# Three quarters of the up projection by Strassen's scheme in a decoder step on one core

## The reference

```python
x = layer_norm(DN_ALPHA * x + cross_attn(x, mem_k, mem_v, xq_w, xo_w), ln2_g, ln2_b)
f = jnp.square(jax.nn.relu(x @ w1 + b1)) @ w2 + b2      # w1 1024 x 4096, w2 4096 x 1024
x = layer_norm(DN_ALPHA * x + f, ln3_g, ln3_b)
```

## Time and profile before

| | us |
|---|---|
| three runs, median | 1382.69 |
| lowest and highest | 1379.11, 1385.63 |
| profiled execution, its own time | 1379.41 |
| its span | 1377.6 |
| PE busy in it | 1326.0 |
| first up slab's Relus to the last one's | 655.1 to 1010.2 |
| down units, first and last matmul with 264 columns | 1009.9 to 1264 |

### The profile page before, as it was taken

The page is one execution under the profiler, slowest core; times in us unless marked ns, Lnnn a source line. Parts: engine busy times, 40 slices in busy tenths (PEclk is TensorE's granted clock), DMA queues, the critical chain, the costliest instruction groups (busy, mean ns, idle before and its releaser), DMA issues.

```text
span 1377.6 us, 21845 instructions
## 1 busy us (share of the span) xinstructions
PE 1326.0 (96%) x8744; PEld 1279.3 (93%) x8744; DVE 882.5 (64%) x1034; ACT 431.9 (31%) x821; POOL 783.7 (57%) x576
## 2 busy tenths in 40 slices
PE   6999999999999999999999999999999999989995
PEld 6999988788899978889999999999999999989995
DVE  5899994456612762387664246324469998897767
ACT  4223442245612441145211131112243444422233
POOL 3476987544933714629433337333359999994522
PEclk9999999989999999999999999999999999999998
DMA  8222452110020266201233433333343133346112
GB/s 257 69 51 45 126 162 78 31 46 1 32 61 31 76 234 239 80 16 46 79 93 93 156 93 93 93 93 140 140 162 109 58 110 125 110 158 206 57 47 81
DMA packets 59018, 136.91 MB, mean 99 GB/s; under 512 B 21568, under 2 KB 27968, under 8 KB 56512
## 3 DMA queue, kind: packets, MB, share of 16 engines
q1 hardware_dynamic: 49184, 132.99, 29.7%
q10 hardware_dynamic: 9760, 2.93, 0.9%
HBM read 107.02 MB, written 28.88 MB: 99 GB/s over the span
## 4 chain that ended last, share of the span: by engine, by line
PE 62%; DVE 27%; issue 3%; POOL 3%; DMA 2%; ACT 2%; SPq 0%; DVEq 0%; ACTq 0%; POOLq 0%
PE bank L809 20%; PE bank L810 19%; PE bank L811 19%; DVE bank L1901 11%; DVE ffn_sum L2404 2%; POOL w_low L759 2%; DVE form_low L2372 1%; DVE weight_sums L2388 1%; DVE product_sums L2404 1%; DMA form_full<-hidden 1%; DVE bank L2028 1%; DVE x_full L2018 1%; DVE x_full L2035 1%; DVE form_full L2366 1%; ACT x_full L1613 1%
## 5 line engine op out<-in xcount | busy, mean ns | idle before, releaser
L809 PE MATMUL bank<-x_high,w_high 128*128 128x384 f32 (+1 forms) x1200 | 391.0, 326 | 14.5 <-POOL w_low L475 11.3
L810 PE MATMUL bank<-x_low,w_high 128*128 128x384 f32 (+1 forms) x1200 | 388.3, 324 | 0.0
L811 PE MATMUL bank<-x_high,w_low 128*128 128x384 f32 (+1 forms) x1200 | 387.6, 323 | 0.0
L809 PEld LDWEIGHTS bank<-x_high,w_high 128*128 128x128 f32 x1200 | 226.0, 188 | 17.0 <-POOL w_low L475 10.1
L473 POOL TENSOR_TENSOR w_high<-w_raw,ones 128x1024 fp32r<-128x1024 f32 x48 | 92.0, 1916 | 240.4 <-issue 128.9
L811 PEld LDWEIGHTS bank<-x_high,w_low 128*128 128x128 f32 x1200 | 226.1, 188 | 0.0
L810 PEld LDWEIGHTS bank<-x_low,w_high 128*128 128x128 f32 x1200 | 226.1, 188 | 0.0
L2435 DVE TENSOR_TENSOR relu<-relu 128x384 f32<-128x384 f32 (+1 forms) x96 | 96.6, 1010 | 187.6 <-ACT relu L1807 187.6
L809 PE MATMUL bank<-form_high,w_high 128*128 128x264 f32 x672 | 192.5, 286 | 5.1 <-DVE product_sums L2404 2.0
L810 PE MATMUL bank<-form_low,w_high 128*128 128x264 f32 x672 | 191.5, 285 | 0.0
L811 PE MATMUL bank<-form_high,w_low 128*128 128x264 f32 x672 | 190.5, 283 | 0.0
(11 more groups left out here) (285 smaller groups left out, 2698.9 us busy)
## 6 DMA issues: line engine op xcount, KB each, us to landing
w_raw<-slabs_in SPq DMA_DIRECT2D x110, 512.0 KB, 3.7
dec_kv<-dec_kv_in SPq DMA_DIRECT2D x16, 1024.0 KB, 6.0
hidden<-relu SPq DMA_DIRECT2D x24, 528.0 KB, 5.3
form_full<-hidden SPq DMA_DIRECT2D x24, 528.0 KB, 6.6
mix<-hidden SPq DMA_DIRECT2D x16, 528.0 KB, 5.7
hidden<-relu_low SPq DMA_DIRECT2D x8, 528.0 KB, 3.9
hidden<-unit_high SPq DMA_DIRECT2D x8, 528.0 KB, 4.9
scratch<-slabs_in SPq DMA_DIRECT2D x8, 512.0 KB, 3.9
```

The source lines that it names most:

```text
L809: pe.matmul(out, w_high, x_high, start=first, stop=False)
L810: pe.matmul(out, w_high, x_low, start=False, stop=False)
L811: return pe.matmul(out, w_low, x_high, start=False, stop=last)
```

## The change

24 of the 32 up blocks are now made by 12 units (`VU`) of Strassen's scheme: two output blocks by two halves of x's eight blocks by two halves of the columns. Each unit has seven products, each 2 x 4 x 3 = 24 matmuls with 264 columns; all seven products of a unit land in pairs of banks, and DVE and ACT put the four quarters of the two blocks together from them (`up_unit`, `up_copy`, `up_relu`). Four forms of x (`xs_full`, `xs_high`, `xs_low`, each 4 x 528 = 2112 columns) are made once, in the region of the old attention output. The other eight blocks (24 to 31) go by whole slabs, four ahead of the units and four behind; all eight are split into high and low as before. The preparation of the sum buffer and of the first forms moves to the last four blocks. Weights of the units come as two raw slabs (two halves of the rows), in forms of 512 columns with four slots.

```diff
-LATE = LAST - NU
+VU = (UP - NB) // 2
+V_ST = S_FF + NB
+S_UP, S_FB = S_FF + 4, S_FF + 4 + 2 * VU
+LATE = LAST - NU - 2 * VU
+UP_ORDER = (0, 5, 1, 2, 3, 4, 6)
+UP_READ, UP_SUM = {0: 1, 1: 2, 3: 3, 5: 4, 6: 5}, {2: 2, 4: 4}
+X_FORM = {2: 0, 1: 1, 3: 2, 4: 3}
...
+    xs_high = at("x_form_high", [P, 4, 4, HT], f32r, O_Q)
+    xs_low = at("x_form_low", [P, 4, 4, HT], f32r, O_Q + 16 * HT * 4)
+    xs_full = at("x_form_full", [P, 4, 4, HT], f32, O_Q + 16 * HT * 4)
...
+    def x_quarter(ap, i):
+
+        k, t = {0: (0, 0), 5: (4, 0), 3: (0, HT), 6: (4, HT)}[i]
+        return ap[:, k:k + 4, t:t + HT]
...
         def hidden_out(j):
 
             p = j % 2
-            sp.wait_ge(sem("square"), squared(j + 1))
-            block = relu[:, p, :] if j < KEPT else relu_low[:, p, :].bitcast(f32)
-            sp.dma_start(hidden[:, j, :], block).then_inc(sem(f"hidden_out{p}"), 16)
-            if j >= KEPT:
-                sp.dma_start(hidden[:, j + NB, :], unit_high[:, p, :].bitcast(f32)).then_inc(sem(f"hidden_out{p}"), 16)
+            sp.wait_ge(sem("square"), squared(j) + 4)
+            sp.dma_start(hidden[:, KEPT + j, :], relu_low[:, p, :].bitcast(f32)).then_inc(sem(f"hidden_out{p}"), 16)
+            sp.dma_start(hidden[:, UP + j, :], block_high(j).bitcast(f32)).then_inc(sem(f"hidden_out{p}"), 16)
+
+        def pair_out(V):
+
+            for p, n in ((1, 3), (0, 4)):
+                sp.wait_ge(sem("square"), squared(4) - 4 * VU + 4 * V + n)
+                sp.dma_start(hidden[:, 2 * V + p, :], relu[:, p, :]).then_inc(sem(f"hidden_out{p}"), 16)
...
             if G == 0:
+                sp.wait_ge(sem("st_done"), 7 * VU)
                 for p in range(2):
-                    sp.wait_ge(sem(f"hidden_out{p}"), 32)
+                    sp.wait_ge(sem(f"hidden_out{p}"), pairs_out(VU - 1))
...
-        for j in range(UP):
-            if j < UP - 2:
-                load_next(S_FF + 4 + j)
+        hidden_out(0)
+        load_next(S_UP)
+        load_next(S_UP + 1)
+        for j in range(1, 4):
             hidden_out(j)
-            if j == 9:
+        for V in range(VU):
+            for p in range(2):
+                sp.wait_ge(sem("w_form_low"), 7 * V + 5 + p)
+                sp.wait_ge(sem("weight_sums"), 4 * (V + 1))
+                load(S_UP + 2 * V + 2 + p, p)
+            pair_out(V)
+        for j in range(4, NB):
+            sp.wait_ge(split_done, S_FF + j + 1)
+            load(S_FB + j - 2, j % 2)
+            if j == 4:
                 forms_in(0)
+            hidden_out(j)
...
+        pool.wait_ge(used, S_FF)
+        pool.wait_ge(sem("x_norm_low"), 6 * NB)
+
+        def x_part(out, x, y, op):
+            pool.tensor_tensor(out, x, y, op).then_inc(sem("x_parts"), 1)
+
+        x_part(xs_full[:, 0], x_quarter(xl, 3).bitcast(f32), x_quarter(xl, 6).bitcast(f32), ALU.add)
+        x_part(xs_full[:, 2], x_quarter(xl, 0).bitcast(f32), x_quarter(xl, 3).bitcast(f32), ALU.subtract)
         split(S_FF + 3, 1, S_FF // 2 + 1, MEM_SLABS, freed=S_XO + 8)
+        pool.wait_ge(sem("x_parts"), 2)
+        x_part(xs_full[:, 2], xs_full[:, 2], x_quarter(xh, 0).bitcast(f32), ALU.add)
+        pool.wait_ge(sem("x_parts"), 3)
+        x_part(xs_full[:, 2], xs_full[:, 2], x_quarter(xh, 3).bitcast(f32), ALU.subtract)
+
+        def up_low(f):
+
+            pool.wait_ge(sem("w_form_high"), f + 1)
+            pool.tensor_tensor(wl_up[:, f % 4, :], up_source(f // 7, UP_ORDER[f % 7]), wh_up[:, f % 4, :].bitcast(f32), ALU.subtract)\
+                .then_inc(sem("w_form_low"), 1)
+
+        for f in range(3):
+            up_low(f)
+        pool.wait_ge(sem("form_high"), 3)
+        pool.tensor_tensor(xs_low[:, 3], xs_full[:, 3], xs_high[:, 3].bitcast(f32), ALU.subtract).then_inc(sem("form_low_pool"), 1)
+        for f in range(3, 7 * VU):
+            up_low(f)
...
-        splits(S_FF + 4, S_FF + 18)
-        form_low(0, 0)
-        form_low(0, 4)
-        splits(S_FF + 18, S_FF + 20)
+        for j in range(4, NB):
+            if j < 6:
+                pool.wait_ge(sem("st_done"), 7 * VU - 2 + 2 * (j - 4))
+            split(S_FF + j, j % 2, (S_FB + j - 4) // 2, MEM_SLABS, freed=S_FF + 4 if j < 6 else S_FF + j - 1)
+            if j == 6:
+                form_low(0, 0)
+                form_low(0, 4)
         form_low(0, 5)
         form_low(0, 6)
-        splits(S_FF + 20, S_ST)
...
-        pairs("W1", S_FF, 1, UP // 2, x_parts)
+        pairs("W1", S_FF, 1, 2, x_parts)
+
+        def up_product(f):
+
+            V, q = divmod(f, 7)
+            i, k = UP_ORDER[q], f % 4
+            pe.wait_ge(sem("w_form_low"), f + 1)
+            if V == 0 and i in X_FORM:
+                pe.wait_ge(*((sem("form_low_pool"), 1) if i == 4 else (sem("form_low_dve"), {1: 1, 2: 2, 3: 3}[i])))
+            if f < 4:
+                for n in (2 * k, 2 * k + 1):
+                    take(n, FREED["UP"][n])
+            else:
+                v, r = divmod(f - 4, 7)
+                if r in UP_READ:
+                    pe.wait_ge(sem("up_read"), 5 * v + UP_READ[r])
+                else:
+                    pe.wait_ge(sem("up_sums"), 7 * v + UP_SUM[r])
+            high, low = (xs_high[:, X_FORM[i]], xs_low[:, X_FORM[i]]) if i in X_FORM else (x_quarter(xh, i), x_quarter(xl, i))
+            for c in range(2):
+                t = slice(c * HT // 2, (c + 1) * HT // 2)
+                for kb in range(4):
+                    w = slice(kb * P, (kb + 1) * P)
+                    last = product(ps[2 * k + c][:, 0:HT // 2], wh_up[:, k, w], wl_up[:, k, w], high[:, kb, t], low[:, kb, t],
+                                   kb == 0, kb == 3)
+            last.then_inc(sem("st_done"), 1)
+
+        for f in range(7 * VU):
+            up_product(f)
+        pe.wait_ge(sem("up_read"), 5 * VU - 1)
+        pe.wait_ge(sem("up_sums"), 7 * VU - 3)
+        pairs("W1B", S_FF + 4, 0, 2, x_parts)
...
+        def up_block(j):
+
+            p, stage, turn = j % 2, "W1" if j < 4 else "W1B", j % 4 // 2
+            for c, (a, z) in enumerate(CHUNKS):
+                b = slab_arrived(act, stage, S_FF + j, p, c, turn)
+                if c == 0 and j >= 2:
+                    act.wait_ge(sem(f"hidden_out{p}"), units_out(j - 2) if j not in (4, 5) else pairs_out(VU - 1))
+                act.activation(relu[:, p, a:z], ps[b][:, 0:z - a], ACT.Relu, bias=col("b1", KEPT + j)).then_inc(free[b], 1)
+            act.wait_ge(sem("square"), squared(j) + 3)
+            act.copy(block_high(j), relu[:, p, :]).then_inc(sem("unit_high"), 1)
+
+        def x_high(k, done):
+
+            act.wait_ge(*done)
+            act.copy(xs_high[:, k], xs_full[:, k]).then_inc(sem("form_high"), 1)
+
+        def up_high(f):
+
+            V, q = divmod(f, 7)
+            i = UP_ORDER[q]
+            if f < 4:
+                act.wait_ge(used, S_FF + 3 + f // 2)
+            else:
+                act.wait_ge(sem("st_done"), f - 3)
+            if i in (0, 5, 4):
+                act.wait_ge(*up_raw(V, 0 if i == 0 else 1))
+            else:
+                act.wait_ge(sem("weight_sums"), 4 * V + {2: 1, 3: 2, 1: 3, 6: 4}[i])
+            act.copy(wh_up[:, f % 4, :], up_source(V, i)).then_inc(sem("w_form_high"), 1)
+
+        def up_copy(V):
+
+            act.wait_ge(sem("st_done"), 7 * V + 1)
+            if V:
+                act.wait_ge(sem("up_sums"), 7 * (V - 1) + 2)
+            act.copy(by_banks(up_part[:, 0, :]), pair(7 * V)).then_inc(sem("up_read"), 1)
+
+        def up_relu(V, q, n, p, a):
+
+            act.wait_ge(sem("up_sums"), 7 * V + n)
+            if q in (1, 3):
+                act.wait_ge(sem(f"hidden_out{p}"), pairs_out(V - 1))
+            act.activation(by_banks(relu[:, p, a:a + HT]), pair(7 * V + q), ACT.Relu, bias=col("b1", 2 * V + p))\
+                .then_inc(sem("up_read"), 1)
+
+        for j in range(4):
+            up_block(j)
+            if j == 1:
+                x_high(0, (sem("form_sums"), 1))
+            if j == 2:
+                x_high(1, (sem("form_sums"), 2))
+                up_high(0)
+                up_high(1)
+        x_high(3, (sem("form_sums"), 3))
+        up_high(2)
+        x_high(2, (sem("x_parts"), 4))
+        up_high(3)
+        for f in range(7 * VU):
+            V, r = divmod(f, 7)
+            if f + 4 < 7 * VU:
+                up_high(f + 4)
+            if r == 0:
+                up_copy(V)
+            elif r == 1:
+                up_relu(V, 1, 1, 0, 0)
+            elif r == 4:
+                up_relu(V, 3, 5, 1, HT)
+            elif r == 5:
+                up_relu(V, 5, 6, 1, 0)
+            elif r == 6:
+                up_relu(V, 6, 7, 0, HT)
+        for j in range(4, NB):
+            if j == NB - 1:
                 for i in range(4):
                     w_form_high(0, i)
-            for c, (a, z) in enumerate(CHUNKS):
-                b = slab_arrived(act, "W1", S_FF + j, p, c, j // 2)
-                if c == 0 and j >= 2:
```

(119 more changed lines are left out.)

95 lines of the change are left out of this document (53 added, 42 removed).

## The result

The changed kernel takes 1415.32 us (median of 4, 1414.77 to 1416.85) against 1382.87 (4 runs) for the one before on the same chip: ratio 1.0238, interval 1.0213 to 1.0264. Its profiled execution took 1415.29, span 1413.5.

A forecast was written before the change was run, and what follows sets the result against it. PE, busy 96% of the span, was taken as the bound. 1379.4 - 32 (units) + 41 (x forms) + 0 (inside units) + 31 (last blocks) = 1419.4, said as 1420 us; own range 1400 to 1440, chance 0.64.

The forecast's parts named there:

- The gain: Up units: 20.6 us each against 23.24 for two up slabs, so twelve units save 32 us.
- How DVE and POOL meet: DVE instructions with both inputs in SBUF and POOL's take turns under an exclusive lock, so both engines' times add up.
- the 1 us late that I had named: Before the units: split of slab 3 ends at 674.2, with block 3 due at 673.3.
- Part 1: Making the x forms before the units: product 3 starts 39.5 us late; cost 41 us, bounds 32 and 46.
- Part 2: Inside the up units: DVE, POOL and their shared path fit under 20.6 us; cost nothing, at most 4 us.
- Part 3: Last four blocks, which take the moved preparation: block 7 and product 4 late; cost 31 us, bounds 11 and 40.
- The late add_product(0): Last blocks: first product added only after DVE's sum_sets 6 and 7, about 82 us after the last unit product.
- The clock term: Half clock after PE stalls: each costs another 1.7 us before the units, 1 us at the last blocks.
- Rival 3: Units bound by DVE too, 22 us each, tail at 40, 1446 us; chopped products at half rate, up to 10 more; chance 0.11.
- Rival 1: DVE and POOL overlap enough, and the four blocks cover both stretches; 1358 us; chance 0.13.
- Rival 2: Half the stalls, as queues find gaps around POOL's long x additions: 21 + 16, 1384 us; chance 0.12.
- Rival 4: The change doesn't do what it says; the prediction saw no such case and gave no chance.

The follow-up runs named there:

- x_parts_on_vector: Against the changed kernel, DVE makes all ten additions and the lows of the x forms, POOL none; 1400.93 us, ratio 1.0133.
- relus_of_block_2_first: Against the changed kernel, ACT's queue takes block 2's Relus and the first two weight highs ahead of the first x high copy; 1410.38 us, ratio 1.0201.
- split_7_first: Against the changed kernel, POOL's two form lows ahead of block 7's weight split go behind it; 1413.09 us, ratio 1.0211.
- last_blocks_rearranged: Against the changed kernel, six sum_sets in the units, two before block 4, form sums and highs a block earlier, split 7 before POOL's form lows; 1394.43 us.

## Why the prediction was right, point by point

**The gain: 34, forecast 32.** A unit takes 20.41 us, not 20.6, and 12 x (23.24 - 20.41) = 34.0. The 122.4 ns a matmul of the earlier trace rows came from a window of down units that holds two waits of 0.24 us; in the up units, without waits, it is 121.5.

**How DVE and POOL meet: as read.** The earlier trace rows had two pairs. After has a whole stretch of them (timelines of DVE and of POOL):

```profile
660.91 3.94 DVE L2608 TENSOR_TENSOR relu<-relu 128x288 f32<-128x288 f32 x1 [1.95 <-ACT relu L1915]
666.00 4.60 DVE L2613 TENSOR_TENSOR relu_low<-relu,early_high 128x1056 fp32r<-128x1056 f32 x1 [1.15 <-ACT early_high L1917]
670.52 9.85 DVE L2608 TENSOR_TENSOR relu<-relu 128x384 f32<-128x384 f32 x3
681.51 4.58 DVE L2613 TENSOR_TENSOR relu_low<-relu,early_high 128x1056 fp32r<-128x1056 f32 x1 [1.14 <-ACT early_high L1917]
686.02 2.34 DVE L2686 TENSOR_TENSOR x_form_full<-x_form_full,x_high 128x2112 f32<-128x2112 f32 x1
```
```profile
659.77 9.71 POOL L801 TENSOR_TENSOR x_form_full<-x_low 128x2112 f32<-128x2112 f32 x2
669.45 2.90 POOL L524 TENSOR_TENSOR w_high<-w_raw,ones 128x1024 fp32r<-128x1024 f32 x1
672.43 2.60 POOL L526 TENSOR_TENSOR w_low<-w_raw,w_high 128x1024 fp32r<-128x1024 f32 x1
674.99 9.99 POOL L801 TENSOR_TENSOR x_form_full<-x_form_full,x_high 128x2112 f32<-128x2112 f32 x2
```

A square of 288 columns, which takes 0.45 at 703.52 with POOL idle, ends at 664.85, just after POOL's first x_part; the block low of 1.26 takes 4.60, and the first x addition starts at 686.02, behind the block low that POOL's last x_part (until 684.98) had held up. Both block lows end 1.1 us after a POOL addition (until 669.48 and 684.98), as the one of 3.44 in the earlier trace rows does. In this whole stretch POOL's list decides when DVE's ends, and between 686 and 707.5 POOL stands still for DVE's and ACT's results. The rule of the Trainium skill that the prediction cited, SBUF — State Buffer, section Who interferes with whom, a lock held for an instruction, is what these rows and x_parts_on_vector show.

I had named only instructions with both inputs in SBUF. That was too narrow: a TENSOR_SCALAR of the sum_sets reads one tensor from SBUF, takes 0.76 alone, and had a median of 2.90 in the earlier trace rows already. In after it stands still beside POOL's form lows like the others (timelines of DVE and of POOL):

```profile
1018.01 2.96 DVE L2672 TENSOR_SCALAR ffn_sum<-x_high,params 128x1056 f32<-128x1056 f32 x1
...
1014.31 6.10 POOL L829 TENSOR_TENSOR form_low<-form_full,form_high 128x1056 fp32r<-128x1056 f32 x2
```

The split of block 3 ended at 675.03, when it was due, so the 1 us late that I had named did not occur.

**Part 1: 37, forecast 41.** The last x addition ends at 703.61 (forecast 704.9), product 0 starts at 708.88 (710.4) and product 3 at 729.78 (733.2), although everything began 1.6 us later. So product 3 was 3.4 us ahead of my mark and 5 with the later start taken off; the difference is spread, and no single step of the order was wrong. Of the 37, 30.3 are idle and 6.6 are seven products that take 27.0 us instead of 20.4 (4.45, 3.08, 4.96, 5.45, 3.27, 2.92, 2.90 without their waits).

**Part 2: nothing, as forecast.** Units 1 to 11 are 20.41 us apart to the hundredth, with DVE at 57% and POOL at 52% in the window above.

**Part 3: 28.7, forecast 31.** With t = 968.87, block 7 starts at t + 45.6 (forecast 48.3), the down units at t + 59.5 (61.6), product 4 at t + 78.7 (82.8). The late add_product(0) is the copy of DVE behind sum_sets 6 and 7 (DVE's timeline):

```profile
1037.54 1.26 DVE L2613 TENSOR_TENSOR relu_low<-relu,unit_high 128x1056 fp32r<-128x1056 f32 x1 [1.14 <-ACT unit_high L1917]
...
1045.67 1.11 DVE L2676 TENSOR_TENSOR ffn_sum<-ffn_sum 128x528 f32<-128x528 f32 x1
1046.70 1.31 DVE L2575 COPY product_sums<-bank 128x528 f32<-128x528 f32 x2
```

8 us of sum_sets stand between the block low and that copy, in a queue with PE at its end. DVE's 45.7 busy us between 968.9 and 1028.4 hold some 15 in which it stood still beside POOL (an estimate: durations above what the same instructions take alone, as 7.35 for three squares that take 1.39). How much of the 28.7 that makes no run says; only part 1 was run with POOL's work taken away. Waits are 23.3 of the 28.7 and the half clock 5.4: block 7 runs 13.87 us instead of 11.62, the first group of down units 56.97 instead of 41.32 with 12.71 of waits in it. My marks were 2 to 4 us late, each of them.

**The clock term: too small.** The windows of after around the stalls (columns as above, granted clock third from the end):

```profile
708.90:712.00 3.10, 3.10 (x14) 3.10 (x15) 3.07 (x3) 0.41 (x2) 1.61 (x1) 0.50 0.31 124
712.00:716.30 4.30, 4.30 (x36) 4.20 (x35) 4.30 (x4) 0.00 (x0) 0.00 (x0) 0.99 0.00 0
...
721.80:725.00 3.20, 3.20 (x14) 3.20 (x15) 2.69 (x1) 2.48 (x5) 3.20 (x1) 0.50 0.29 118
...
732.00:735.00 3.00, 3.00 (x15) 3.00 (x15) 0.00 (x0) 0.00 (x0) 1.90 (x2) 0.50 0.84 254
...
738.50:741.40 2.90, 2.90 (x26) 2.90 (x25) 1.43 (x2) 1.32 (x2) 1.30 (x1) 1.00 0.00 0
...
1031.40:1036.00 4.60, 3.53 (x27) 3.35 (x28) 4.50 (x8) 0.78 (x2) 1.32 (x2) 1.00 0.00 0
```

Each of the five stalls of 3.05 to 21.90 us brought the clock down to 1.2 GHz (granted clock 0.50), and it stayed there for a while after PE had work again: 3.2 us from 708.88, 3.9 from 721.77, 6.2 from 729.78, 4.8 from 1014.48, 5.9 from 1047.54. That is 24.0 us of work at half rate, so 12 lost (6.6 in part 1, 5.4 in part 3); the waits of 1.49 and 1.01 brought none (last row). It is also why PE's busy time fell by only 21.3 us where the units save 34. Not all 12 are on the path, though: products 0 to 2 at half rate only shorten the wait for product 3, whose start POOL sets, and relus_of_block_2_first, where product 0 ran at full rate, brought unit 1 forward by 2.2 us alone. What counts in full is the work behind the last stall of each part: 3.1 us behind 729.78 (half of 6.2) and 2.9 behind 1047.54, where I had taken 1.7 and 1 from the 3.5 us of the earlier trace rows. This is the term of the sum that was sized wrong, by 3.3 us, and the marks that came early hid it. Rival 3 had all eleven chopped products at half rate, and that is not so: products 1, 5 and 6 of unit 0 took 3.08, 2.92 and 2.90, the full rate's 2.92. Nor did its "up to 10 us" have a working: eleven products are 7 x 24 + 4 x 12 = 216 matmuls, and at 0.22 us each instead of 0.12 they would be some 21 us longer before the stalls hide any of it. The Trainium skill, TensorE: Matmul & The Clock Gate, section A second HAM failure mode: psum-queue depth-cycling, which the prediction cited there, says that gaps between matmul groups take the clock up and down, and these windows show that.

**The rivals.** Rival 1 (overlap, 1358) falls by the rows above and by x_parts_on_vector. Rival 2 (half the stalls, 1384) would have lost 37 us in both parts, and 66 were lost. Rival 3 (units bound by DVE, 1446) falls by 20.41. Rival 4 was none: 84 products of 24 matmuls ran (9032 matmuls, 288 more than before, as 84 x 24 is more than 24 x 72). The sum is 5 us off because errors went both ways: 2 more gained, 6 less lost in parts 1 and 3, and 4 us (1.6 ahead of the change, 2.6 in blocks 0 to 3, the later down units and the end) that I had no term for.

That the total came within 5 us is partly luck, since these errors offset each other in part; the three terms that carry it were each within 4 us.

## What to carry to other kernels

Where DVE and POOL hold a shared port in turns, as here for the DVE instructions without an input in PSUM, add up both lists before a deadline, with the slower engine's price for what it does; work given to the slower engine is then not taken off the faster one, it makes the path longer. Moved work has to be put where PE has cover per stretch, not on average: six sum_sets cost nothing in the units, where DVE is 57% busy, and 10 us in the last blocks. And reordering one queue that has too much ahead of a deadline moves the wait, whereas less work or an earlier place removes it: split_7_first alone gave 2 us, and last_blocks_rearranged, which takes sum_sets out of the stretch and moves the forms up, 21.

## What the runs showed of the hardware that I had not expected

The clock came back and fell again with every stall, instead of staying at one level through a chopped stretch: in 50 us it was down from 691.6 to 712.1, from 718.9 to 725.7 and from 729.2 to 736.0, each time from 2.5 to 4.6 us after PE had fallen idle. The shortest of these stalls, 3.05 us, was followed by the most work at half rate, 6.2 us, against 3.2 after the longest of 21.90, and 3.6 after the 2.27 of the earlier trace rows. What decides between 3.2 and 6.2 the rows don't show. Nor did I expect that a wait of 3 us would be followed by as much lost to the clock.
